# Four-layer hybrid network step: the state-space scan with one merged mixing matrix and inputs turned a group ahead, and a scatter that no longer waits for the next copy

## What is computed

```python
def ssd_scan(x, dt, a, bm, cm, h0):          # called forward, and on flipped inputs
    a_cs = jnp.cumsum(dt * a.reshape(SSD_GROUPS, hpg), axis=2)
    dtx = x * dt[..., None]
    seg = a_cs[:, :, :, None] - a_cs[:, :, None, :]
    decay = jnp.exp(jnp.where(lower, seg, -jnp.inf))
    cb = jnp.einsum('bclgn,bcsgn->bclsg', cm, bm)
    y_diag = jnp.einsum('bclsg,bclsgh,bcsghp->bclghp', cb, decay, dtx)
    chunk_states = jnp.einsum('bclgn,bclgh,bclghp->bcghpn', bm, decay_to_end, dtx)
    y_off = jnp.einsum('bclgn,bcghpn,bclgh->bclghp', cm, h_prev, jnp.exp(a_cs))
...
    y = y_f + _flip(y_b) + d_skip.astype(jnp.float32)[:, None] * x.astype(jnp.float32)
...
def hier_moe(h, ...):
    act = jax.nn.silu(hg) * hu * combine[:, :, None].astype(t.dtype)
    return jnp.einsum('tef,efd->td', act, w_down).reshape(h.shape)
```

## Time and profile before

| what | us |
|---|---|
| median of 3 runs | 1855.09 (1854.03 to 1857.5) |
| the profiled execution, its own time | 1851.99 |
| its span | 1850.2 |
| PE busy | 1736.1 (94%) |
| DVE busy | 529.3 (29%) |
| ACT busy | 364.9 (20%) |
| POOL busy | 102.0 (6%) |
| mean traffic from and to memory | 332 GB/s |

### The profile page before, as it was taken

How to read it: one execution, slowest core, us unless ns; L and a number is a source line. 1 busy time by engine, 2 the same in 40 slices (tenths; PEclk the granted TensorE clock), 3 DMA queues, 4 the chain that set the end, 5 groups by cost and what they waited for, 6 DMA issues and landing times.

```text
span 1850.2 us, 20985 instructions
## 1 busy us (share of the span) xinstructions
PE 1736.1 (94%) x8810; PEld 910.1 (49%) x8810; DVE 529.3 (29%) x1159; ACT 364.9 (20%) x671; POOL 102.0 (6%) x171
## 2 busy tenths in 40 slices
PE   5999999999999999999998999999999999799995
PEld 2444344367544434334864444435786754434441
DVE  1131221320531222130033021224245892312123
ACT  2031011121331101120202111113223651201111
POOL 1000000000000000000000000000002840000000
PEclk9999999999899999999999999999999999899998
DMA  9999999998369999899447999997855566599991
GB/s 384 361 423 427 426 427 425 391 340 310 114 236 408 424 425 426 360 379 343 170 169 278 397 427 422 428 402 280 324 187 165 159 200 241 214 428 426 427 426 76
DMA packets 92850, 614.10 MB, mean 332 GB/s; under 512 B 7504, under 2 KB 7728, under 8 KB 51408
## 3 DMA queue, kind: packets, MB, share of 16 engines
q1 hardware_dynamic: 85584, 585.36, 78.2%
q0 software_dynamic: 7168, 27.33, 4.7%
HBM read 608.34 MB, written 4.33 MB: 331 GB/s over the span
## 4 chain that ended last, share of the span: by engine, by line
PE 84%; DVE 6%; DMA 4%; ACT 3%; issue 2%; POOL 0%; SPq 0%; DVEq 0%; POOLq 0%; ACTq 0%
PE psum L1073 23%; PE psum L594 14%; PE psum L587 12%; PE psum L1108 12%; PE psum L1055 6%; PE psum L1124 6%; PE psum L653 4%; DMA arena<-in_fnet_w_o 2%; DMA ring<-in_ada_w 1%; DMA ring<-in_moe_w_down 1%; DVE arena L1786 1%; PE psum L1093 1%; PE psum L691 1%; PE psum L968 1%; ACT arena L1440 1%
## 5 line engine op out<-in xcount | busy, mean ns | idle before, releaser
L1073 PE MATMUL psum<-ring,arena 128*64 128x512 f32 x1152 | 343.2, 594 | 0.0
L587 PE MATMUL psum<-at,ring 128*128 128x256 f32 x1024 | 223.6, 380 | 0.0
L587 PEld LDWEIGHTS psum<-at,ring 128*128 128x128 f32 x1024 | 193.7, 190 | 28.4 <-issue 1.6
L1073 PE MATMUL psum<-arena 128*64 128x512 f32 x608 | 190.1, 594 | 0.2 <-issue 0.2
L1073 PEld LDWEIGHTS psum<-ring,arena 128*64 128x64 f32 x1152 | 107.7, 137 | 165.1 <-issue 165.1
L1853 DVE TENSOR_TENSOR outtmp<-psum,gate 128x512 f32<-128x512 f32 x128 | 87.7, 685 | 349.1 <-PE psum L1124 349.1
L1108 PE MATMUL psum<-ring,arena 128*64 128x512 f32 x624 | 184.6, 598 | 2.6 <-DMA ring<-in_moe_w_down 2.6
L594 PE MATMUL psum<-ring,at 128*128 128x512 f32 (+1 forms) x416 | 172.5, 569 | 0.4 <-DVE at L1704 0.4
L1124 PE MATMUL psum<-arena 128*128 128x512 f32 x256 | 117.6, 602 | 25.0 <-ACT arena L1440 13.6
L1844 DVE TENSOR_TENSOR arena<-arena,psum 128x512 f32<-128x512 f32 x32 | 33.9, 1060 | 365.8 <-PE psum L1073 365.8
L1055 PE MATMUL psum<-arena,xn 128*128 128x128 f32 x1024 | 126.4, 284 | 6.4 <-issue 6.4
(11 more groups left out here) (254 smaller groups left out, 1553.7 us busy)
## 6 DMA issues: line engine op xcount, KB each, us to landing
ring<-in_ada_w SPq DMA_DIRECT2D x43, 2048.0 KB, 9.8
ring<-in_moe_w_down SPq DMA_DIRECT2D x39, 2048.0 KB, 17.4
ring<-in_moe_w_up SPq DMA_DIRECT2D x38, 2048.0 KB, 13.7
ring<-in_moe_w_gate SPq DMA_DIRECT2D x34, 2048.0 KB, 16.8
arena<-in_moe_w_gate SPq DMA_DIRECT2D x22, 2048.0 KB, 13.1
arena<-in_moe_w_down SPq DMA_DIRECT2D x17, 2048.0 KB, 16.1
arena<-in_moe_w_up SPq DMA_DIRECT2D x16, 2048.0 KB, 14.8
ring<-in_ssd_w_in SPq DMA_DIRECT2D x12, 2048.0 KB, 9.4
```

The costliest lines, as they stand in the source:

```text
L587: last = nc.tensor.matmul(dst, slot(k)[:, c, m * P:(m + 1) * P], src[:, c, :], start=(c == 0), stop=(c == nk - 1))
L1073: last = nc.tensor.matmul(ps[b][e * CAP:(e + 1) * CAP, :], rows, slot_half(k + e, 4, h)[:, c, :], start=(h == 0 and c == 0), stop=(h == 1 ...
```

## The change

**Scatter.** The wait for `xg_ev` is kept for pairs 6 and 7 and left out for pairs 0 to 5.

**Scan, the arithmetic.** The two decays are made as one: since the forward exponent is below zero where the backward one is above it and the other way round, the smaller of the two is the right one at each place. DVE takes it in four instructions a group instead of eight, each with two matrices as inputs (L1796 of the changed kernel), and ACT takes the exponential in four pieces of 128 x 128 with the rest of the exponent as its bias (L1407). The step size dt moves from the inputs `dtx` into the mixing matrix: POOL masks B·C (L539) and multiplies the backward part by dt for all four heads (L542, 128 x 512, `mixw`), DVE adds the forward part (L1803, four instructions) and multiplies by the decays once (L1807) instead of twice. PE then needs one product a head (L966) instead of two, straight from `xtok`. `dtx` is gone; `dtxw` is made from `xtok` with a factor worked out once (L1778); L1776 to L1778 are three small instructions ahead of the scan.

**Scan, the order.** `xtok` has four buffers instead of two. PE makes the inputs of group i+1, and ACT copies them, one iteration sooner than before. The DMAs of POOL for the given state and the output states stand behind its arithmetic instead of ahead of it.

```diff
-        segs = carve(12288, 4, 512)
+        segs = carve(12288, 2, 512)
+        mixw = carve(13312, 2, 512)
...
-        xtok = acc[:, 0, :].rearrange("p (u n) -> p u n", u=2)
+        xtok = acc[:, :, :].rearrange("p s (u n) -> p (s u) n", u=2)
         cbm = outtmp[:, 1, :].rearrange("p (u n) -> p u n", u=4)
-        dtx = acc[:, 1, :].rearrange("p (u n) -> p u n", u=4)
...
+                        for d in range(2):
+                            last = pool.tensor_tensor(cbm[:, t + d, :], xtok[:, u % 4, 384:512], tri[d], ALU.mult)
+                        last.then_inc(cb_masked, 1)
+                        pool.wait_ge(cb_masked, u + 1)
+                        pool.tensor_tensor(heads(mixw[:, u % 2, :]), cbm[:, t + 1, :].unsqueeze(1).to_broadcast([P, HPG, P]),
+                                           W2(7)[:, s, hs[1]].unsqueeze(2).to_broadcast([P, HPG, P]), ALU.mult).then_inc(cbw_ready, 1)
+                        if s == 0:
+                            for d in range(2):
+                                last = pool.tensor_tensor(heads(dtxw[:, t + d, :]), heads(xtok[:, u % 4, 0:256]), over(W2(6)[:, 0, hs[d]]), ALU.mult)
+                            last.then_inc(dtx_ready, 1)
...
                         for h in range(HPG):
-                            for d in range(2):
-                                last = nc.tensor.matmul(ps[3][:, h * HD:(h + 1) * HD], segs[:, t + d, h * P:(h + 1) * P],
-                                                        dtx[:, t + d, h * HD:(h + 1) * HD], start=(d == 0), stop=(d == 1))
+                            last = nc.tensor.matmul(ps[3][:, h * HD:(h + 1) * HD], segs[:, u % 2, h * P:(h + 1) * P],
+                                                    xtok[:, u % 4, h * HD:(h + 1) * HD], start=True, stop=True)
...
+                    group_inputs(0)
                     for i in range(S * SG + 1):
-                        if i < S * SG:
-                            group_inputs(i)
+                        if i + 1 < S * SG:
+                            group_inputs(i + 1)
...
-                    pe.wait_ge(xg_ev, 2 * min(G + 3, PAIRS * (n + 1)))
+                    if x >= LAST - 1:
+                        pe.wait_ge(xg_ev, 2 * PAIRS * (n + 1))
...
+                    def operands_copied(u):
+                        act.wait_ge(xt_mm, u + 1)
+                        if u >= 4:
+                            act.wait_ge(yg_mm, u - 3)
+                            act.wait_ge(y_done, u - 3)
+                        A(xtok[:, u % 4, :], ps[0][:, :], ACT.Copy).then_inc(xt_ev, 1)
...
+                            act.wait_ge(seg_ready, i + 1)
+                            for h in range(HPG):
+                                seg = segs[:, i % 2, h * P:(h + 1) * P]
+                                hh = i % SG * HPG + h
+                                last = A(seg, seg, ACT.Exp, bias=adt[:, i // SG, SH + hh:SH + hh + 1])
+                            last.then_inc(dec_ready, 1)
...
+                        for h in range(HPG):
+                            hh = g * HPG + h
+                            last = V.scalar_tensor_tensor(segs[:, u % 2, h * P:(h + 1) * P], rows[:, 0, h, :], adt[:, s, hh:hh + 1], rows[:, 1, h, :],
+                                                          ALU.add, ALU.min)
+                        last.then_inc(seg_ready, 1)
+                        dve.wait_ge(cbw_ready, u + 1)
+                        for h in range(HPG):
+                            hh = g * HPG + h
+                            mw = mixw[:, u % 2, h * P:(h + 1) * P]
+                            last = V.scalar_tensor_tensor(mw, cbm[:, t, :], W2(7)[:, s, hh:hh + 1], mw, ALU.mult, ALU.add)
+                        last.then_inc(mixw_ready, 1)
+                        dve.wait_ge(mixw_ready, u + 1)
+                        dve.wait_ge(dec_ready, u + 1)
+                        V.tensor_tensor(segs[:, u % 2, :], segs[:, u % 2, :], mixw[:, u % 2, :], ALU.mult).then_inc(m_ready, 1)
```

64 lines of the change are left out of this document (21 added, 43 removed).

## The result

The changed kernel takes 1829.12 us in the median of 4 runs (1826.45 to 1830.56), the kernel before 1855.03 (1854.03 to 1857.5). The ratio is 0.9857, 95% interval 0.984 to 0.9874: 25.9 us less, where 26.0 had been forecast; by the interval it is 23.4 to 29.7.

A forecast was written before the change was run, and what follows sets the result against it. PE bounds the kernel, with DMA beside it in expert stages and DVE in the scan's latent half. 13.9 (scatter) + 5.2 + 0.7 + 6.2 (scan) = 26.0 us off 1855.1 gives 1829; range 1822 to 1842.

The forecast's parts named there:

- signs of being wrong: PE's wait for DVE before L606 grows in the latent half, or DMA waits appear in expert layers 1 to 3.
- Scatter, 0.75 a pair: Expert layers: ending PE's wait before six scatters a layer gains 0.75 us each, 4.5 a layer; bounds 0.65 to 0.85.
- The lead of the weights: Pair 6's down load, layer 3, lands 5.0 us before use; 4.5 is paid, 0.5 left; layers 1 and 2 no less.
- Rival (b): Expert layers: weight loads land later and take back the scatter's gain, leaving 0.4 of 13.9 us; 1842.5 us; chance 0.08.
- Layer 0, 0.4: Layer 0's scatter edit gains 0.4 us, not 4.5, since the down load has only 0.5 us of lead.
- Context half, 5.2: Scan's context half: four of PE's eight mix products go, step 6.89 to 6.15 us, gaining 5.2; 2.7 to 6.1.
- rival (c): Scan: POOL's 128 x 512 product is slow in every group's path; at 4.5 us, 1863 us in all; chance 0.03.
- Start of the scan, +0.7: Scan's start: PE's 0.73 us wait for group 0 goes with inputs a group ahead, gaining 0.7 us.
- Latent half, 6.2: Scan's latent half: DVE's step falls from 7.33 to 6.25 us, gaining 6.2 over seven steps; bounds 2.3 to 8.5.
- the whole 0.8: Latent half: at most 0.8 us of POOL's cost a step can land on DVE; 0.35 was taken.
- Rival (a), dear instructions: Scan: new two-input DVE instructions follow every 0.40 us, eight costing 1.3 us more; whole gain 18, 1837 us; chance 0.18.
- the 0.13 of the forecast: Extra us for 128 columns of a new DVE instruction by the skill's half-throughput rule, giving 1835 us in all.

The follow-up runs named there:

- the kernel with the met wait: Changed kernel with an always-met wait for the next pair's copies put back ahead of the scatter; 1829.52 us, ratio 0.9871.
- The kernel with the sooner exponentials: Changed kernel with the differences signalled after two heads and after four, so ACT may start after two; 1826.65 us, ratio 0.985.
- the kernel with the root later: Sooner exponentials and group 1's differences ahead of group 0's sums, plus ACT's context root moved from step 14 to 15; 1821.44 us, ratio 0.9832.
- theory A: For the changed kernel with POOL's latent masks one DVE product later: seven latent steps 1.7 to 3.4 us shorter; measured 1829.33 us, ratio 0.9865.
- half the scatter: Changed kernel with the scatter's products cut from 512 to 256 columns, leaving out half its result; 1823.44 us, ratio 0.9842.

## Why the prediction was right, and where it was not

The sum was 26.0, the ledger says 24.0 and the medians 25.9. So close an agreement is luck in good part: single terms missed by up to 2.4 us, some above and some below, and the profiled executions differ by 2 us less than the medians. Two of the signs of being wrong that I had named did show: PE's wait for DVE ahead of L606 grew in the latent half, from at most 0.25 us a step (group 14 aside) to 0.43, and a wait for DMA appeared in layer 3.

- **Scatter, 0.75 a pair: mis-sized, 0.90, over my upper bound of 0.85.** The mechanism was right (the last rows of the table: the layers of the kernel with the met wait). The bound was drawn in the wrong place. I measured from the start of ACT's copy (1217.87), but that copy waits for the gather's last product to end, and PE had by then started the small transposes L1060 (1217.67), the work right ahead of the scatter. The right measure is from the start of L1060 to the scatter, 1.05, less what the same two need without the wait, 0.22; 0.07 more came inside the scatter.
- **The lead of the weights: the mechanism held, the margin didn't.** The three layers pay 5.3, 5.4 and 4.6; I had seen a lead of 5.0 in layer 3 and said that 0.5 would be left. As the pairs gained more than 0.75, the lead was used up and 0.55 us of wait came. In layers 1 and 2 the leads were 5.9 and 6.1, no less as I had counted on, and 0.5 and 1.4 were left. Rival (b) fell: nothing else was taken back.
- **Layer 0, 0.4: it is nothing that can be told from 0**, for the reason given: PE waits for `moe_w_down` ahead of L1107 instead.
- **Context half, 5.2: 5.6.** PE's own step is 5.99 and the mean step 6.10 (6.02 and 6.15 forecast). POOL's L542 took 1.04 alone, 1.0 forecast, and 1.37 beside DVE: rival (c), which began to hurt at 2.4, fell.
- **Start of the scan, +0.7: wrong, -1.3.** I took the wait of 0.73 us as gone because the inputs come a group ahead. I didn't follow what else comes ahead with them: DVE's differences and sums of group 1 now run beside POOL's products ahead of the gating of group 0, at 2.62 and 1.77 us where 1.13 each was the price, and the wait of 0.73 grew to 1.58. Moving them (12.85 for 14.56) shows it; with the inputs not ahead it is 13.02.
- **Latent half, 6.2: 3.8.** The step was 6.61, not 6.25. By the parts of my sum: differences 1.05 for 1.0; the sums with the wait for ACT 1.50 for 1.25; product 0.85 for 0.68; rest 3.21 for 2.96; and 0.35 that I had set aside for POOL. So POOL's share was sized about right (0.17 + 0.25 = 0.42). The mis-sized term is the second, 0.25 of the 0.36 us by which the step missed, and in it the wait for ACT: four exponentials take 1.28, not 1.14, and ACT starts them 1.17 us after the first difference, since one signal covers all four. The kernel with the sooner exponentials takes that wait out, and the step falls to PE's own 6.06. Around group 14 the wait I had left 0.8 for is real (7.35 there, 0.75 above the others), and it is the root's tables (the kernel with the root later). The two bounds of this term also don't follow from what they name: 50.8 - 7 x 6.0 is 8.8, not 8.5, and the whole 0.8 with 0.05 more on each of eight instructions makes a step of 7.1 and a gain of 0.3, not 2.3. The measured 3.8 lies inside either way.
- **y 14 to y 15: left out.** The mix products of group 15 lie there; four of them went, 0.9 us.
- **Rival (a), dear instructions: no.** The new instruction takes 0.34 us and follows every 0.26, 0.316 and 0.23 forecast; the one-input instruction that it replaces takes 0.34 and follows every 0.26 as well. The rows that answer to the earlier trace rows, by shape (xcount, busy and mean ns of one, which hold the contended ones):

```profile
L1803 DVE SCALAR_TENSOR_TENSOR arena<-outtmp,dtw,arena 128x128 f32<-128x128 f32 x64 | 20.1, 373 | 12.6 <-POOL arena L542 12.6
...
L1796 DVE SCALAR_TENSOR_TENSOR arena<-arena,adt 128x128 f32<-128x128 f32 x32 | 10.5, 387 | 0.0
```

The Trainium skill, Vector Engine (DVE) Microarchitecture Reference, Points that are easy to get wrong, has such an instruction at half throughput when both matrix inputs are in SBUF and not bf16. By that rule it would take some 0.45 us (an estimate from 0.316 and the 0.13 of the forecast); the trace shows 0.34 where POOL is idle, so the rule does not show here.

## What to carry to other kernels

A wait of an engine that is the bound cost more here than its idle time shows (0.90 for 0.67 us): take the distance between the starts of the instructions on either side, and subtract what the same pair needs without it. When work is split into small pieces (four exponentials for one), the signal has to be split too, or the piece next in line starts as late as before. An order and an arithmetic can be worth little until both are there: without the inputs ahead, the new arithmetic brought 1.3 of 9.0 us. And where two limits stand side by side (here PE and the weights, both at a share of about 1.00), read the lead of the last load ahead of the edit: it is about the most that the other engine's edit can gain up to there. Here it was 5.0 us in layer 3, of which 4.6 were gained, and of the next 10.2 us a layer cut from PE, between -0.7 and 1.3 were gained up to that load.

## What the runs showed of the hardware

- DVE and POOL at work at the same time are dearer than I had counted at the start of the scan: four instructions of 128 x 128 with two matrix inputs take 1.13 us alone and up to 2.62 beside POOL's products; POOL's own 128 x 512 product takes 1.04 alone and 1.37 beside them. Moving POOL's masks by one product of DVE only moved the collision (0.3 us gained of the 3.4 that theory A could give). DVE instructions that read a bank were not slowed: beside POOL's product L1816 takes 0.42 and two of L1820 take 0.76, and just as much where POOL makes no product (1507.32 and 1507.77 of the changed kernel), while L1814, with both inputs elsewhere, takes 0.67 for 0.42.
- An ACT instruction with a bias column on 128 x 128 takes 0.39 us, and four in a row 1.28; one exponential on 128 x 512 takes 0.63 (L1401 of the kernel before). Splitting by four doubles the price.
- The granted clock fell to its lower level for some us ahead of y 15 in two of the twelve profiled executions (means of 0.52 and 0.64 over 3 us), which cost 1.7 us each time; in the other kernels with the new scan the stretch comes back at 8.89 or 8.90. With half the scatter it fell in layer 2 behind a wait of 2.3 us in which PE did nothing, and did not fall behind one of 2.6 us in layer 1. Medians of five runs with intervals of 2.5 us can't see an edit of 1.7 us; the stretch between two PE instructions comes back within 0.1.
